# Expert gathers regrouped: 64 tokens times two experts, with 128x64 diagonals in the two column halves of TensorE

## The reference

```python
q = (tb @ w_query).reshape(128, 8, 2, 64)            # tb: a block of 128 tokens, h: 8 heads
s = jnp.einsum('thpd,hpnd->thpn', q, sub_keys)       # 2 x 128 key scores for each head
s1, i1 = lax.top_k(s[:, :, 0], 16)
s2, i2 = lax.top_k(s[:, :, 1], 16)
...                                                  # 16 x 16 sums, and their 16 best: top_s, idx
g = jax.nn.softmax(top_s, axis=-1)
act = gelu(jnp.einsum('thkd,td->thk', expert_u[idx], tb))
out = jnp.einsum('thk,thkd->td', g * act, expert_v[idx])
```

## Time and profile before

| | us |
|---|---|
| median of 3 runs | 3502.38 (3499.14 to 3504.32) |
| the profiled execution | 3508.87 |
| its span, first to last instruction | 3507.1 |
| PE busy | 2937.6 (84%) |
| DVE busy | 2068.5 (59%) |
| ACT busy | 1449.7 (41%) |
| gathers | 1073.81 MB, 76.6% of the 16 DMA engines' span |
| first gather, first dot product, last dot product | 605.2, 619.5, 3491.2 |

### The profile page before, as it was taken

How to read it: one execution, slowest core, us unless ns; L and a number is a source line. 1 busy time by engine, 2 the same in 40 slices (tenths; PEclk the granted TensorE clock), 3 DMA queues, 4 the chain that set the end, 5 groups by cost and what they waited for, 6 DMA issues and landing times.

```text
span 3507.1 us, 34097 instructions
## 1 busy us (share of the span) xinstructions
PE 2937.6 (84%) x8106; PEld 1330.5 (38%) x8106; DVE 2068.5 (59%) x6700; ACT 1449.7 (41%) x3719; POOL 1314.0 (37%) x1198
## 2 busy tenths in 40 slices
PE   8999974698979997898979897987698769876776
PEld 5444433244324532353334433443244324432222
DVE  2021133947955696559755885579557855784444
ACT  3021132536844476337843784323333233323222
POOL 1000010344434443444444444444344434444553
PEclk9988866899999999999989998999899889999999
DMA  3011130999899988998899989999999999999998
GB/s 141 30 49 38 38 120 28 353 387 398 285 362 398 417 304 310 402 407 348 315 399 407 387 303 390 399 419 380 363 398 420 375 367 402 419 374 389 421 422 339
DMA packets 183358, 1131.51 MB, mean 323 GB/s; under 512 B 20368, under 2 KB 44768, under 8 KB 51056
## 3 DMA queue, kind: packets, MB, share of 16 engines
q0 software_dynamic: 147456, 1073.81, 76.6%
q1 hardware_dynamic: 35696, 55.48, 4.5%
HBM read 1114.38 MB, written 14.81 MB: 322 GB/s over the span
## 4 chain that ended last, share of the span: by engine, by line
PE 39%; DVE 28%; DMA 16%; issue 8%; ACT 5%; POOL 3%; POOLq 0%; DVEq 0%; SPq 0%; ACTq 0%
PE ps L1353 18%; DMA r_uv<-in_experts,r_wk 16%; DVE r_uv L1049 9%; DVE r_wk L1003 6%; PE ps L1159 5%; PE ps L1327 3%; PE ps L1310 3%; POOL r_uv L535 3%; PE ps L1115 2%; DVE r_wk L911 2%; DVE r_wk L914 2%; DVE r_wk L920 2%; PE ps L1186 1%; DVE r_wk L917 1%; PE ps L1173 1%
## 5 line engine op out<-in xcount | busy, mean ns | idle before, releaser
L1353 PE MATMUL ps<-r_uv,r_wk 128*128 128x512 f32 x4096 | 1937.0, 621 | 433.4 <-ACT r_wk L739 432.7
L535 POOL DMA_INDIRECT r_uv<-in_experts,r_wk x1024 | 1201.0, 1173 | 1679.8 <-PE ps L1353 1385.5
L1049 DVE CUSTOM_DVE_ANT_0 r_uv<-r_uv,hncur 128x1024 f32<-128x1024 f32 x1024 | 1241.9, 1233 | 730.4 <-DMA r_uv<-in_experts,r_wk 723.8
L1353 PEld LDWEIGHTS ps<-r_uv,r_wk 128*128 128x128 f32 x4096 | 775.0, 197 | 1506.0 <-issue 904.7
L729 ACT ACTIVATE r_wk<-r_wk 128x2 f32<-128x2 f32 x512 | 104.0, 203 | 1384.1 <-DVE r_wk L1049 1383.2
L739 ACT ACTIVATE r_wk<-cst,r_wk 128x128 f32<-128x128 f32 x1024 | 355.5, 394 | 82.7 <-PE ps L1353 42.4
L735 ACT ACTIVATE r_wk<-r_wk 128x1 f32<-128x1 f32 x1024 | 245.9, 287 | 17.3 <-ACT r_wk L729 0.2
L1003 DVE SCALAR_TENSOR_TENSOR r_wk<-cst,r_wk 128x50 f32<-128x50 f32 x1024 | 224.4, 287 | 2.3
L1159 PE MATMUL ps<-r_uv,r_wo 128*128 128x512 f32 (+1 forms) x448 | 178.9, 560 | 3.7 <-DVE r_wk L831 3.7
L729 ACT ACT_TABLE_LOAD x135 | 173.2, 1283 | 18.2 <-issue 15.8
L563 ACT ACT_TABLE_LOAD x130 | 166.8, 1283 | 4.6 <-issue 0.2
(11 more groups left out here) (155 smaller groups left out, 2061.0 us busy)
## 6 DMA issues: line engine op xcount, KB each, us to landing
r_uv<-in_experts,r_wk POOLq DMA_INDIRECT x1024, 10.9
r_wo<-in_w_pair SPq DMA_DIRECT2D x4, 1536.0 KB, 7.5
r_uv<-in_x SPq DMA_DIRECT2D x8, 512.0 KB, 3.6
r_wk<-in_x SPq DMA_DIRECT2D x8, 512.0 KB
r_wo<-in_w_out SPq DMA_DIRECT2D x1, 4096.0 KB, 14.8
r_wq<-in_w_query SPq DMA_DIRECT2D x1, 4096.0 KB, 23.8
r_wk<-lkv_dram SPq DMA_DIRECT2D x32, 128.0 KB, 8.7
result<-h2cur SPq DMA_DIRECT2D x8, 512.0 KB, 8.0
```

The source lines that it names most:

```text
L535: g.indirect_dma_start(uv[:, k % NB, :], None, experts, bass.IndirectOffsetOnAxis(idxcur_u[:, k:k + 1], 0)).then_inc(rows_in[k % NB], 16)
L1049: v.tensor_tensor_reduce(uv[:, k % NB, 0:D], uv[:, k % NB, 0:D], hncur[:, :], 1.0, 0.0, ALU.mult, ALU.add, actv[:, k:k + 1]).then_inc(dott ...
L1353: last = t_.matmul(ps[:, i, :], diag[:, k % 4, :], uv[:, k % NB, D + 512 * i:D + 512 * i + 512], start=k == 0, stop=k == K - 1)
```

## The change

A gather no longer holds one expert of 128 tokens but two experts of 64 tokens. For a pair of experts (2m, 2m+1), gather k = 2m + j serves token half j: partitions 0 to 63 receive expert 2m of these 64 tokens, partitions 64 to 127 expert 2m + 1 of the same tokens. A matmul with a 128x64 matrix, which has the weights of expert 2m on the diagonal of its upper 64 rows and those of expert 2m + 1 on that of its lower 64, then adds both experts into 64 rows of the sum: rows 0 to 63 for j = 0, rows 64 to 127 for j = 1. Four of these matmuls (2 column parts of v times 2 token halves) take the place of four with a 128x128 diagonal.

- The indices and gates have to be rearranged in this way: `spread`, four 64-partition copies for one copy. The tokens are needed twice: `repeat_rows` writes `hnrep` (2 x 1024 values, each half on all partitions) with four 64-partition copies for the one that filled `hncur`.
- The gates no longer multiply the Gelu on ACT. `gate_columns(c)` on DVE forms for 4 experts at a time the 128x64 matrices that have the gates on their diagonals (128x256 values, one instruction, 32 in a tile), and ACT scales them by the Gelu (new L739), 128x64 for each expert, and writes them over the first 64 values of the spent u.
- PE waits once for a pair, for both matrices, and its order is j within i.
- Small memory: `pos` and `topi` now share the words of their float copies, and other buffers are packed closer.

```diff
@@ ACT, experts_of @@
-                    link(a.activation(gel[:, GRP * n:GRP * n + GRP], actv[:, GRP * n:GRP * n + GRP], ACT.Gelu))
...
+                    link(a.activation(actv[:, GRP * n:GRP * n + GRP], actv[:, GRP * n:GRP * n + GRP], ACT.Gelu))
+                    if n % GRP == 0:
+                        act.wait_ge(gated_ready, NG // GRP * b + n // GRP + 1)
                     for k in range(GRP * n, GRP * n + GRP):
-                        last = a.activation(gel[:, k:k + 1], gel[:, k:k + 1], ACT.Copy, scale=gcur[:, k:k + 1])
-                    link(last)
-                    act.wait_ge(rows_used, K * b + GRP * n + GRP - 4 + NB)
-                    for k in range(GRP * n, GRP * n + GRP):
-                        a.activation(diag[:, k % 4, :], ident, ACT.Copy, scale=gel[:, k:k + 1]).then_inc(diag_ready, 1)
+                        a.activation(uv[:, k % NB, 0:HALF], gated[:, k // GCH % 2, k % GCH, :], ACT.Copy,
+                                     scale=actv[:, k:k + 1]).then_inc(diag_ready, 1)
@@ DVE @@
+            def spread(into, of, n0, n1):
+                for q in range(GRP):
+                    for j in range(GRP):
+                        last = v.tensor_copy(
+                            into[HALF * q:HALF * q + HALF, n0:n1].rearrange("p (m j) -> p m j", j=GRP)[:, :, j],
+                            of[HALF * j:HALF * j + HALF, n0:n1].rearrange("p (m q) -> p m q", q=GRP)[:, :, q])
+                return last
+            def gate_columns(c):
+                form = [P, GCH, HALF]
+                v.tensor_tensor(gated[:, c % 2, :, :], ident64.unsqueeze(1).to_broadcast(form),
+                                gcur[:, GCH * c:GCH * c + GCH].unsqueeze(2).to_broadcast(form), ALU.mult
+                                ).then_inc(gated_ready, 1)
+            def repeat_rows():
+                for q in range(GRP):
+                    for j in range(GRP):
+                        last = v.tensor_copy(hnrep[HALF * q:HALF * q + HALF, j, :], hnn[HALF * j:HALF * j + HALF, :])
+                return last
@@ DVE, head_experts and head_gates (tile 0) @@
-                v.tensor_copy(idxcur_u[:, TOPK * h:TOPK * h + TOPK], idxf3[:, h, :]).then_inc(head_ready, 1)
+                spread(idxcur_u, idxf, TOPK * h, TOPK * h + TOPK).then_inc(head_ready, 1)
...
-                v.tensor_scalar(gcur3[:, h, :], gn3[:, h, :], gsum[:, h:h + 1], None, ALU.mult
-                                ).then_inc(gates_ready, 1)
+                link(v.tensor_scalar(gn3[:, h, :], gn3[:, h, :], gsum[:, h:h + 1], None, ALU.mult))
+                link(spread(gcur, gn, TOPK * h, TOPK * h + TOPK))
@@ DVE, experts_of @@
-                    v.tensor_copy(idxcur_u[:, K // 2:K], idxn_u[:, K // 2:K]).then_inc(idx_ready, 1)
-                    link(v.tensor_copy(hncur[:, :], hnn))
+                    spread(idxcur_u, idxf, K // 2, K).then_inc(idx_ready, 1)
+                    repeat_rows()
...
-                    v.tensor_copy(gcur, gn).then_inc(gates_ready, 1)
+                    link(spread(gcur, gn, 0, K))
+                    gate_columns(0)
...
+                    if n % GRP == GRP - 1 and n < NG - 1:
+                        dve.wait_ge(diag_ready, K * b + GRP * n - GRP)
+                        gate_columns(n // GRP + 1)
@@ PE, experts_of @@
-                        pe.wait_ge(diag_ready, K * b + k + 1)
-                        for i in range(2):
-                            last = t_.matmul(ps[:, i, :], diag[:, k % 4, :],
-                                             uv[:, k % NB, D + 512 * i:D + 512 * i + 512], start=k == 0,
-                                             stop=k == K - 1)
-                        last.then_inc(rows_used, 1)
+                    pe.wait_ge(diag_ready, K * b + GRP * n + GRP)
+                    for i in range(2):
+                        for j in range(GRP):
+                            k = GRP * n + j
+                            last = t_.matmul(ps[HALF * j:HALF * j + HALF, i, :], uv[:, k % NB, 0:HALF],
+                                             uv[:, k % NB, D + 512 * i:D + 512 * i + 512], start=n == 0,
+                                             stop=n == NG - 1)
+                            if i == 1:
+                                last.then_inc(rows_used, 1)
```

66 lines of the change are left out of this document (34 added, 32 removed).

## The result

The changed kernel takes 3519.57 us (median of 5 runs, 3518.44 to 3533.35) where the kernel before takes 3500.54 beside it (3499.1 to 3504.32). The ratio is 1.005, 95% interval 1.0034 to 1.0066: slower by 12 to 23 us. The forecast was 3489, the range ended at 3519. The profiled execution took 3519.27 us, span 3517.5, against 3508.87 and 3507.1: between the two traces lie only 10.4 us, less than between the medians, because the trace of before lies 8.3 us above the median of these runs and that of after on its own.

What follows compares the result with a forecast made beforehand. Transfers were taken to bound the plain case, other engines certain stretches, with only 327 us of lost queue time partly winnable. Terms -24 -17 -10 +22 +10 +8 -2 = -13 took 3508.9 to 3495.9, less 6.5: 3489 us, range 3463 to 3519.

Steps and rivals of the forecast that it cites:

- Term 1: Mix stretches, experts 24 to 47 of tiles 0 to 6: TensorE's pair takes 1.88 us instead of 3.44; -24 us.
- term 2: ScalarE drops gate products and halves diagonals, saving about 0.65 us a pair; 4.3 us in each of four tiles, -17.
- term 3: Buffers released on average 1.2 us earlier, before searches and at tile 0's start, so the queue runs dry later; -10 us.
- Term 4: VectorE's new gate products, 0.36 us each, count in full for 62 where VectorE is the bound; +22 us.
- Term 5: Tile 0's start, VectorE busy throughout: more copies, waits and gate products; +10 us.
- Term 6: Seven tile changes: VectorE's copies cost +3.0 us each, partly offset by an earlier last pair; +8 us.
- Term 7: End of the last tile, with none following: only the last pair counts; -2 us.
- Rival B: TensorE idles longer between shorter pairs and its clock falls; 3514 us at worst, 3502 likelier; chance 0.17.
- Rival A: VectorE pays more than it gets, with products at 0.64 us and copies at 1.3 us; 3527 us, chance 0.20.
- rivals C and D: C: TensorE's halves don't run side by side, 3542 us, chance 0.05. D: the queue gains more, 3453, chance 0.10.

Runs made afterwards that it cites:

- Experiment 7: The kernel before, without ScalarE's two gate products for each pair from k104 to k120 of every tile; ratio 1.0002 to the kernel before.
- experiment 11: Changed kernel with zero-weight matmuls, also k92 to k120 in tiles 0 to 3, and gates multiplied on ScalarE from k72 to k104; ratio 0.9958 to the kernel before.
- experiment 9: Changed kernel with gates multiplied in on ScalarE from k72 to k104 alone, by VectorE's products elsewhere; ratio 1.0005 to the kernel before.
- experiment 3: Changed kernel with tile 0's heads copying indices and gates in one instruction each, without moves to the other half; ratio 1.0026 to the kernel before.
- experiment 8: Changed kernel with one copy of each kind (indices, rows, gates) at a tile change in place of four; ratio 0.9994 to the kernel before.
- experiment 1: Changed kernel with four zero-weight matmuls behind each pair that no next-tile step or late attention unit follows; ratio 1.0002 to the kernel before.

## Why the prediction was wrong

It said 3489, faster; measured are 3520, slower. Between the traces it said -13, and 10.4 are measured. Of these 23 us some 17 lie in tiles 0 to 3 between k72 and k128 and 6 at the start of tile 0. By the account of the queue, against the steps:

- **Term 1, the mix stretches, -24: right.** 30.4 to 5.7 us lost, -24.7, and pairs of 1.94 us. Pair and mix step take 5.50 us where the sum had 5.3, and the buffers take that up: the mix stretch of tile 6 runs at 422 GB/s. The Trainium skill (TensorEngine Tiling (Array Packing), Key Properties) says that a change of tiling mode drains the engine; the trace leaves room for a small cost only, these 0.2 us for the two changes around a step beside what the 1.88 us already held.
- **Terms 2, 3 and 4 in tiles 0 to 3: this is the step that failed.** The terms give -17 from ScalarE, -5.6 of the earlier release, +11.5 for products, -11 in all; measured are +5.5. What failed is term 2's sentence that ScalarE "saves about 0.65 us for a pair" and "where it is the bound" this is 4.3 us for a tile. It took ScalarE for the bound of a stretch in which its own row shows TensorE busier (46.99 us against 45.11 of 50.09), and the stretch isn't what sets the end: the rows that come in between k104 and the next tile do. Experiment 7 makes most of this saving and nothing else: in tile 1 ScalarE is busy 3.3 us less between k104 and k120, the stretch gets shorter, and the experts behind it get it back. The queue loses 1.0 us less there in the four tiles, the ratio is 1.0002. Without term 2 the other two give +5.9. That this meets the +5.5 is partly luck, since term 3 did not come either; what else keeps the queue empty in these stretches stays open, and with clock and products both mended (experiment 11) 5.2 us are won against the kernel before, not 11. The prediction measured what the queue loses and then priced a gain by an engine's time; its own figure, 15 us lost in that window, was not asked again for the window behind it.
- **Term 3, the earlier release, -10: not there.** The lower clock is not the reason in tiles 4 to 6: with it up again and the products off VectorE (experiment 11) they lose 31 us, where 30.0 were lost before the change. The reason stays open. The term was also too large by its own rows: 2.2 us for the second buffer adds 1.88, the new pair's length, to 0.32, where the pair gets 3.44 - 1.88 = 1.56 shorter.
- **Term 4 in tiles 4 to 6: about right.** +10.8, or +6.6 with term 3's part; measured +8.7, and experiment 9 takes 7.9 of it away. The product is 0.433 us long (0.425 forecast).
- **Term 5, tile 0's start, +10: too small.** Lost time +13.9, and the first dot product 5.3 later with 1.35 more experts loaded, +2, which is within what the same code varies by: +16. The head in the timeline of experiment 3 costs 1.74 us more, not 0.9: a copy that moves 64 partitions takes some 0.18 us from start to start even with 8 values, where I took 0.1 from the earlier trace rows.
- **Term 6, tile changes, +8: right in sum, its parts both larger.** Measured +13.7 in k0 to k8 and -4.8 in k8 to k24. VectorE's part is 3.6 us for each, 3.0 forecast, and fully on the path (experiment 8: 20 us). What came back was taken too large here too (2.2 us for 1.9), and 7.3 us of the lost time go with the clock (experiment 1).
- **Term 7, -2:** -1.4. These parts are +13.0; other transfers took 2.6 less, which gives the 10.4.
- **From the profile to the median.** 6.5 us were taken off because the trace of before lay above its median. That of after doesn't, so this is part of the miss: 10.4 us between the traces, 17.5 by the ratio. The five runs of before also have a lower median than any of its later sets.

Rival B, with a chance of 0.17, is a mechanism that the changed kernel does show: mean clock 0.815, pairs that alternate between 1.94 and 3.48 us, and 17 us back by the ratios (12 by the traces) when the engine is kept busy. Its worst case, 3514, was still below the result, since it kept term 2. The Trainium skill (TensorE: Matmul & The Clock Gate, HAM oscillation) says that short bursts with waits between them swing between both clocks; the four pairs of tile 7 agree, and in the prediction this rule should have weighed more than the single harmless gap of 1.26 us. Rival A's prices did not come (0.433 for 0.64 us), rivals C and D are out.
